# Differential attention on one core: ScalarE's copies in a head's last two steps are issued ahead of its exponentials

## The reference

```
DIFF_HEADS = 8
DIFF_HEAD = D_MODEL // (2 * DIFF_HEADS)      # 64
Q_BLOCK = 128
...
    def one_block(args):
        qblk, start = args
        s = jnp.einsum('bqhcd,bkhcd->bhcqk', qblk, k).astype(jnp.float32) * scale
        qpos = start + jnp.arange(Q_BLOCK)
        mask = kpos[None, :] <= qpos[:, None]
        s = jnp.where(mask, s, -jnp.inf)
        p = jax.nn.softmax(s, axis=-1)
        attn = p[:, :, 0] - lam * p[:, :, 1]
        return jnp.einsum('bhqk,bkhe->bqhe', attn.astype(v.dtype), v)
...
    o = rmsnorm(o, subln_w, SUBLN_EPS) * (1.0 - lam_init)
    return o.reshape(B, L, D_MODEL).astype(h.dtype) @ w_out
```

## Time and profile before

| | us |
|---|---|
| median of 3 runs | 3435.7 |
| the profiled execution: its own time | 3424.8 |
| its span in the profile | 3422.7 |
| PE busy in the span | 3060.1 (89%) |
| DVE busy | 1388.7 (41%) |
| POOL busy | 1085.1 (32%) |
| ACT busy | 991.8 (29%) |
| the chain that ended last, PE's share | 70% |
| mean granted clock of PE, share of full speed | 0.948 |
| the attention stage, first matmul to the last head's out-copy | 2787.2 to 2951.4 |

### The profile page before, as it was taken

The page is one execution under the profiler, slowest core; times in us unless marked ns, Lnnn a source line. Parts: engine busy times, 40 slices in busy tenths (PEclk is TensorE's granted clock), DMA queues, the critical chain, the costliest instruction groups (busy, mean ns, idle before and its releaser), DMA issues.

```text
span 3422.7 us, 43448 instructions
## 1 busy us (share of the span) xinstructions
PE 3060.1 (89%) x17026; PEld 2503.7 (73%) x17026; DVE 1388.7 (41%) x2236; ACT 991.8 (29%) x1578; POOL 1085.1 (32%) x724
## 2 busy tenths in 40 slices
PE   6887899898999899989888887799997978879997
PEld 4665467776885787867788876699996846658886
DVE  5786354402055213031575533550603054355252
ACT  2222343223122353212442211222222224432221
POOL 0332112443331693444321100143432320124443
PEclk9999999999999999999999977899998989989998
DMA  4986011344732693323220001122222200013332
GB/s 136 269 268 211 25 38 55 106 151 145 218 112 86 156 249 111 94 68 97 69 62 14 2 1 31 50 92 87 92 91 65 81 13 1 31 56 98 93 95 78
DMA packets 130693, 324.77 MB, mean 95 GB/s; under 512 B 54096, under 2 KB 54736, under 8 KB 129760
## 3 DMA queue, kind: packets, MB, share of 16 engines
q1 hardware_dynamic: 95904, 221.29, 21.6%
q0 software_dynamic: 30272, 88.88, 9.3%
q10 hardware_dynamic: 4352, 12.25, 0.9%
HBM read 288.38 MB, written 33.95 MB: 94 GB/s over the span
## 4 chain that ended last, share of the span: by engine, by line
PE 70%; DVE 16%; DMA 4%; ACT 3%; POOL 3%; issue 2%; DVEq 0%; ACTq 0%; POOLq 0%
PE ps L237 16%; PE ps L240 16%; PE ps L242 15%; PE ps L247 3%; DMA d_pb<-arena 3%; DVE h L546 2%; PE ps L2270 2%; POOL ring_r L323 1%; PE ps L526 1%; DVE inv L538 1%; PE ps L2281 1%; PE ps L589 1%; PE ps L1820 1%; PE ps L1834 1%; PE ps L1183 1%
## 5 line engine op out<-in xcount | busy, mean ns | idle before, releaser
L323 POOL TENSOR_TENSOR ring_r<-ring,high 128x1024 fp32r<-128x1024 f32 x330 | 834.0, 2527 | 1628.5 <-ACT high L331 1628.3
L237 PE MATMUL ps<-h_hi,high 128*128 128x512 f32 (+1 forms) x2144 | 749.2, 358 | 65.9 <-DVE h_r L551 40.6
L242 PE MATMUL ps<-h_hi,ring_r 128*128 128x512 f32 (+1 forms) x2144 | 674.9, 350 | 0.0
L240 PE MATMUL ps<-h_r,high 128*128 128x512 f32 (+1 forms) x1952 | 660.3, 348 | 0.0
L331 ACT ACTIVATE high<-ring 128x1024 fp32r<-128x1024 f32 x362 | 381.9, 1055 | 611.1 <-PE ps L237 486.3
L237 PEld LDWEIGHTS ps<-h_hi,high 128*128 128x128 f32 x2144 | 411.4, 192 | 146.7 <-issue 71.4
L242 PEld LDWEIGHTS ps<-h_hi,ring_r 128*128 128x128 f32 x2144 | 379.8, 192 | 54.4
L240 PEld LDWEIGHTS ps<-h_r,high 128*128 128x128 f32 x1952 | 376.9, 193 | 42.0 <-issue 1.0
L240 PE MATMUL ps<-f_r,high 128*128 128x264 f32 (+1 forms) x832 | 261.2, 326 | 0.0
L237 PE MATMUL ps<-f_hi,high 128*128 128x264 f32 (+1 forms) x768 | 236.6, 321 | 0.0
L237 PE MATMUL ps<-z_hi,high 128*128 128x512 f32 x488 | 199.1, 408 | 31.0 <-POOL ring_r L323 30.7
(11 more groups left out here) (417 smaller groups left out, 4663.5 us busy)
## 6 DMA issues: line engine op xcount, KB each, us to landing
ring<-in_units SPq DMA_DIRECT2D x402, 512.0 KB, 3.6
d_ca<-arena POOLq DMA_DIRECT2D x16, 640.0 KB, 8.9
arena<-d_ca POOLq DMA_DIRECT2D x16, 640.0 KB, 6.6
arena<-d_q POOLq DMA_DIRECT2D x32, 256.0 KB, 8.1
d_pb<-arena POOLq DMA_DIRECT2D x16, 512.0 KB, 11.1
arena<-d_pb POOLq DMA_DIRECT2D x16, 512.0 KB, 4.0
arena<-d_ca POOLq DMA_DIRECT2D x16, 512.0 KB, 5.2
arena<-d_k POOLq DMA_DIRECT2D x128, 64.0 KB, 4.6
```

Of the source, the lines that this page charges most:

```text
L237: part = mm(acc, hi[:, cols], self.x_hi(k)[:, t0:t0 + tn], start=(k == 0), stop=False)
L240: mm(acc, hi[:, cols], self.x(k)[:, t0:t0 + tn], start=False, stop=False)
L242: ins = mm(acc, w[:, cols], self.x_hi(k)[:, t0:t0 + tn], start=False, stop=(k == self.kt - 1))
L323: eng.tensor_tensor(b.ring_r[:, slot, :], b.ring[:, slot, :], self.high[:, j % 2, :], ALU.subtract).then_inc(b.unit_lo, 1)
```

## The change

Only ACT's stream in the attention stage changes. The bodies of power and keep become two local functions, and the loop calls them in an order that depends on n modulo 4:

- where n % 4 is 2 or 3, keep(n-2) is issued ahead of power(n); where it is 0 or 1, behind it as before;
- where n % 4 is 3, the out-copy of the head that mix(n-4) ended comes first of all, ahead of keep(n-2) and power(n). The squares stay behind them.

The numbers of instructions, their shapes, their waits and the semaphores' counts are the same as before, and the streams of PE, DVE, POOL and SP are the same.

```diff
         for n in range(self.steps + 4):
+            keep_first = n % 4 >= 2
+            if n >= 4 and n % 4 == 3:
+                act.wait_ge(self.mixed, n - 3)
+                f(m.o[:, n // 4 - 1, :, :], b.ps[:, 7, :].rearrange("p (t e) -> p t e", t=4), ACT.Copy
+                  ).then_inc(self.out_kept, 1)
+            if keep_first and n < self.steps + 2:
+                keep(n - 2)
             if n < self.steps:
...
+                power(n)
+            if not keep_first and 2 <= n < self.steps + 2:
+                keep(n - 2)
             if n >= 4 and (n - 4) % 4 == 3:
                 h = (n - 4) // 4
-                act.wait_ge(self.mixed, n - 3)
-                f(m.o[:, h, :, :], b.ps[:, 7, :].rearrange("p (t e) -> p t e", t=4), ACT.Copy).then_inc(self.out_kept, 1)
                 act.wait_ge(self.out_kept, h + 1)
                 if h:
                     act.wait_ge(b.squared, self.at["squared"] + 4 * h)
                 for t in range(4):
                     f(m.t_sq[:, t, :], m.o[:, h, t, :], ACT.Square, accum_out=m.squares[:, 4 * h + t:4 * h + t + 1]
                       ).then_inc(b.squared, 1)
```

## The result

| | before | after |
|---|---|---|
| median, us | 3435.9 (4 runs, 3434.5 to 3436.2) | 3391.4 (4 runs, 3389.6 to 3394.1) |
| ratio | | 0.989, 95% interval 0.9868 to 0.9913 |
| the profiled execution, us | 3424.8 | 3389.6 |
| attention stage, first matmul to the start of the last out-copy | 163.6 | 130.0 |
| in it: first matmul to score(7) | 22.5 | 24.4 |

The account below looks back on a forecast made before the run. PE waiting at seven head ends for ACT's out-copy was taken to bound the kernel; 23.9 us of waiting plus 11.7 us of clock, 35.6 us, off 3435.7 gave 3400 us, range 3396 to 3412.

Parts of the forecast that it names:

- What bounds the kernel: Attention stage, head ends: PE waits for ACT's out-copy, held behind the exponentials though its data are ready; seven waits, 24.5 us.
- The first term, 23.9 us: Seven head ends: mix(8) starts 3.57 us sooner, less a new 0.15 us wait; net 3.42 us each, 23.9 us.
- the new one for the scale: At each head end, turn(10) would wait 0.15 us for DVE's scale(10), including some 0.05 us for the signal.
- the walk: Step-by-step timing of the engines from score(11) on, with a head of 15.46 us against 20.47.
- The second term, 11.7 us: Without the long wait PE's clock stays full at the seven head ends, saving 11.7 us; lower bound 0.
- The copies of the turned probabilities ahead: On ACT, keep(n-2) before power(n) fits idle time; counted as nothing, or 1.0 us in the first head without cover.
- The spare times: On ACT and DVE behind power(11): scale(11) has 0.8 us or more to spare, mix(10) 1.2 us or more.
- rival 2: ACT's stream becomes late as keep(9) delays the exponentials; a 1.8 us slip costs 7 us in all, 3407; chance 0.06.
- From the profiled execution to the median: Whole kernel: the runs' median lies 10.9 us above the profiled execution; carried over unchanged, giving 3400 us from 3389.2.
- Rival 1: Attention stage: the wait goes but the clock still falls once a head; 3412 us, chance 0.07.
- Rival 3: Attention stage: uninterrupted small matmuls hold PE at 1.2 GHz for good; slower, 3481 us, chance 0.04.
- Rival 4: Nothing comes of it: out-copy not ahead, or something behind the stage was due then anyway; 3436 us, chance 0.03.

Follow-up runs that it names:

- r1_copy_only: Changed kernel with only the out-copy ahead of the exponentials, the other copies behind them as in the kernel before; 3391.1 us, ratio 0.990 to the kernel before.
- r3_fill: Kernel before plus 12 unread 128x128 matmuls on PE at each of the seven head ends, ahead of the out-copy wait; 3413.7 us, ratio 0.996.
- r2_slip3: Changed kernel plus three idle 128x1024 copies on ACT ahead of the exponentials of steps 7, 11 and so on to 31; 3404.1 us (one run).
- r2_copy_mid: Changed kernel with the out-copy between the exponentials of the two score maps of step 4h+3; 3423.4 us, ratio 0.999 to the kernel before.
- r3_after: Changed kernel, unchanged, run again for a second profile; 3392.9 us (one run).

## Why the prediction came out as it did

**What bounds the kernel.** Right. The out-copy waited for its place in ACT's stream. With it alone in front, the 24.5 us of waiting were gone (r1_copy_only).

**The first term, 23.9 us.** Right but for the last end. The wait is gone, and the new one for the scale is 0.13 us against 0.15; the 0.05 us for the signal stood there without a source, and the trace has 0.05 (the scale ends at 2829.88, turn(10) starts at 2829.93). The head is 15.46 us, as in the walk. At the last end there is no score in front of the turn, PE is there 0.4 us sooner and waits 0.51 us, which the term left out.

**The second term, 11.7 us.** Right, and shown by itself in r3_fill (10.8 to 11.7 us). The Trainium skill, on the page "TensorE: Matmul & The Clock Gate", section "A second HAM failure mode: psum-queue depth-cycling", describes a bf16 kernel with N=512 that cycles through PSUM banks, where frequent micro-idles of PE let the clock swing. I let that speak against the term, and the clock stayed at 1.00. But it was hardly put to the test: PE of the changed kernel idled once a head, for 0.13 us at most. With 0.53 us once a head (r3_fill) and with 1.05 and 0.38 us (r2_slip3) the clock stayed up too. It fell behind waits of 2.19 us at six of seven ends (r2_copy_mid) and behind one of 2.16 us (r2_slip3); the section gives no length to hold these against.

**The copies of the turned probabilities ahead.** Right that they cost nothing: power(11) starts at t = 3.50 as before, and in the first head, where keep(0) was to hold power(2), the stage up to score(7) took 22.5 us in r3_after as in the first profile of the kernel before. That they bring nothing I had not said; half of the diff is without effect.

**The spare times.** Right in size and incomplete. I named scale(11), turn(11) and the later copies as the ones who wait for power(11), and left out score(13), which waits for the bank that power(11) reads. It is wanted at t = 7.4 and power(11) ends at 5.34, so some 2.1 us are free there. In r2_slip3 it was the first to wait. At the forecast it changes nothing, but rival 2's price would have been worked out from the wrong waiter.

**From the profiled execution to the median.** This is the step that failed. I carried the 10.9 us between the profiled execution and the median of three runs over to the changed kernel, as if they belonged to the program. They do not: the medians of the changed kernel (3391.4 and 3391.3) lie 2 us above its profiled execution, not 10.9. For the profiled executions the sum held to 0.4 us (3389.2 against 3389.6), and that close it was luck, since 1.9 us lost in the stage's beginning and 1.6 us won outside the stage nearly cancel; what the sum is about, the seven ends, gave 35.5 us against the first profile of the kernel before and 34.6 against the second. The table of the starts shows a scatter of 20 us ahead of the stage with the same instructions there, and the kernel before had medians of 3435.9, 3429.6, 3427.6 and 3425.1 us on four occasions. So the saving in the medians was 44.5 us on the first occasion and 38.3 on the second, where the stage gives 34 to 36. My three runs before agreed within 2 us and I took that for the width of the measurement; the range should have been wider by this scatter, downwards too. What sets the clock ahead of the stage differently from execution to execution is not known from these runs. That the saving beyond 36 us is all scatter is the reading that they favour, not one that they prove.

**The rivals.** Rival 1, the clock falls all the same: it didn't. Rival 2, ACT late: keep(9) did not delay the exponentials, and a slip of 0.90 us is free. Rival 3, the lower level for good: over the head it was 1.00, and the stream without long waits kept the full clock. Rival 4, nothing comes of it: what follows began 35 us earlier and took as long as before.

## What to carry to other kernels

Where an engine works its stream in order, look for an operation whose data are ready and on which the busiest engine waits, behind one that itself waits for a third engine; moving it ahead fills idle time, and here it cost nothing. Price a wait of TensorE with the slower matmuls behind it, from rows at either level: here 3.5 us of waiting cost 5 us, and shortening the wait to 2.2 us gave back 4 to 5 of some 35 us, while removing it gave back all. And compare stage with stage in the trace, from a point on at which the clock stands at the same level, before a difference of medians is believed: one that goes beyond the stage that was changed may be scatter elsewhere.

## What the runs showed of the hardware

A wait of PE of 2.19 us, once a head, left the clock alone the first time and lowered it behind the six others (0.83 over a head). From the third on the clock lost more there than behind waits of 3.5 us (0.92): 20.53 us a head, where the first, with the same wait and the clock full, took 17.56. A single wait of 2.16 us lowered it too (0.50 behind it, r2_slip3). Waits of 1.05 and 0.38 us, 0.7 us apart, left it at 1.00. Matmuls whose result nobody reads, put into the wait of 3.5 us so that 0.53 us of it were left, kept the clock at 1.00 and made the kernel 0.4% faster.
